# Differential attention: a second set of score banks for a head's second to fourth query tiles, and their minima ahead of the scaling

## The reference

```python
def diff_causal_attention(q, k, v, lam):
    '''q,k: (B,H,2,S,dq); v: (B,H,S,dv); lam: scalar float32. Returns (B,H,S,dv).'''
    scale = DIFF_QK_DIM ** -0.5
    for j in range(S_ // Q_BLOCK):
        lo, hi = j * Q_BLOCK, (j + 1) * Q_BLOCK
        s = jnp.einsum('bhmqd,bhmkd->bhmqk', q[:, :, :, lo:hi], k[:, :, :, :hi]).astype(jnp.float32) * scale
        mask = jnp.arange(hi)[None, :] <= jnp.arange(lo, hi)[:, None]
        p = jax.nn.softmax(jnp.where(mask, s, -jnp.inf), axis=-1)
        pd = p[:, :, 0] - lam * p[:, :, 1]
        outs.append(jnp.einsum('bhqk,bhkd->bhqd', pd.astype(v.dtype), v[:, :, :hi]))
```

## Time and profile before

| | |
|---|---|
| median of 3 runs | 3670.33 us (3666.89 to 3671.85) |
| profiled execution, own time | 3672.77 us |
| its span | 3671.0 us |
| TensorE matmul busy | 3372.6 us, 92% of the span |
| VectorE, ScalarE, GpSimd busy | 1344.2, 753.2, 1186.1 us |
| the attention stage | from 478.0 us (first scores) to 626.7 us (last products) |
| chain that ended last | TensorE 83%, VectorE 12%, ScalarE 3%, issue 2% |

### The profile page before, as it was taken

How to read it: one execution, slowest core, us unless ns; L and a number is a source line. 1 busy time by engine, 2 the same in 40 slices (tenths; PEclk the granted TensorE clock), 3 DMA queues, 4 the chain that set the end, 5 groups by cost and what they waited for, 6 DMA issues and landing times.

```text
span 3671.0 us, 37450 instructions
## 1 busy us (share of the span) xinstructions
PE 3372.6 (92%) x15576; PEld 2704.3 (74%) x15576; DVE 1344.2 (37%) x1653; ACT 753.2 (21%) x1091; POOL 1186.1 (32%) x996
## 2 busy tenths in 40 slices
PE   5967976889989899999999999998997899999997
PEld 4646855778868578878888888886984678888885
DVE  4145055133150540223451111217998662222223
ACT  2220045221120540111210000003442310010011
POOL 3200310325423023334444433343331344433341
PEclk9977999999989899999999999998998999999998
DMA  2100100102221001112111111111111011111111
GB/s 112 54 15 21 46 24 12 58 24 73 77 98 48 11 24 46 58 46 93 47 46 46 46 57 46 46 46 73 49 67 48 24 46 46 46 57 46 46 46 46
DMA packets 31742, 179.63 MB, mean 49 GB/s; under 512 B 3840, under 2 KB 4864, under 8 KB 14720
## 3 DMA queue, kind: packets, MB, share of 16 engines
q1 hardware_dynamic: 18864, 137.37, 10.6%
q10 hardware_dynamic: 12752, 40.42, 2.9%
HBM read 163.10 MB, written 14.68 MB: 48 GB/s over the span
## 4 chain that ended last, share of the span: by engine, by line
PE 83%; DVE 12%; ACT 3%; issue 2%; POOL 0%; DMA 0%; DVEq 0%; ACTq 0%
PE ps L441 48%; PE ps L472 16%; PE ps L498 5%; PE ps L1974 3%; DVE c_out L2398 2%; PE ps L1473 1%; PE ps L774 1%; PE ps L1489 1%; ACT p L944 1%; PE ps L682 1%; PE ps L2025 1%; DVE soft L1179 1%; PE ps L1459 1%; PE ps L321 1%; PE ps L329 1%
## 5 line engine op out<-in xcount | busy, mean ns | idle before, releaser
L538 POOL TENSOR_TENSOR whi<-raw,par 128x512 fp32r<-128x512 f32 x117 | 128.7, 1100 | 1939.3 <-PE ps L441 1477.9
L542 POOL TENSOR_TENSOR wlo<-raw,whi 128x512 fp32r<-128x512 f32 x468 | 695.5, 1486 | 37.3
L441 PE MATMUL ps<-xhi,whi 128*128 128x512 f32 x2016 | 631.7, 395 | 34.0 <-DVE xlo L344 9.5
L441 PE MATMUL ps<-xlo,whi 128*128 128x512 f32 x2016 | 626.6, 392 | 0.0
L441 PE MATMUL ps<-xhi,wlo 128*128 128x512 f32 x2016 | 625.0, 391 | 0.0
L441 PEld LDWEIGHTS ps<-xhi,whi 128*128 128x128 f32 x2016 | 379.8, 190 | 122.6 <-issue 11.9
L441 PEld LDWEIGHTS ps<-xlo,whi 128*128 128x128 f32 x2016 | 382.1, 190 | 81.3
L441 PEld LDWEIGHTS ps<-xhi,wlo 128*128 128x128 f32 x2016 | 381.3, 189 | 81.4
L540 POOL CAST whi<-raw 128x512 fp32r<-128x512 f32 x351 | 279.2, 795 | 0.0
L472 PE MATMUL ps<-hidden_lo,whi 128*128 128x512 f32 x864 | 268.9, 393 | 0.0
L472 PE MATMUL ps<-hidden_hi,whi 128*128 128x512 f32 x864 | 268.3, 392 | 0.4 <-DVE hidden_lo L1334 0.4
(11 more groups left out here) (480 smaller groups left out, 4588.4 us busy)
## 6 DMA issues: line engine op xcount, KB each, us to landing
raw<-stream SPq DMA_DIRECT2D x131, 1024.0 KB, 4.7
x_in<-xT ACTq DMA_DIRECT2D x4, 1024.0 KB, 14.7
x_again<-xT ACTq DMA_DIRECT2D x4, 1024.0 KB, 8.6
h_scr<-x_again ACTq DMA_DIRECT2D x4, 1024.0 KB, 4.3
h<-h_scr ACTq DMA_DIRECT2D x1, 4096.0 KB, 14.6
h_scr<-h ACTq DMA_DIRECT2D x4, 1024.0 KB, 4.7
outT<-h ACTq DMA_DIRECT2D x8, 512.0 KB, 3.0
bias<-bias ACTq DMA_DIRECT2D x1, 2560.0 KB, 9.5
```

Of the source, the lines that this page charges most:

```text
L441: mm = nc.tensor.matmul(ps[:, c0 + c:c0 + c + width], w, x(k, a, width), start=(n == 0 and m == 0), stop=(n == len(ks) - 1 and m == 2))
L538: nc.gpsimd.tensor_tensor(WHI[:, r, t], RAW[:, r, t], one, ALU.mult).then_inc(hi_done, 1)
L542: ins = nc.gpsimd.tensor_tensor(WLO[:, r, t], RAW[:, r, t], WHI[:, r, t].bitcast(F32), ALU.subtract)
```

## The change

The scores of the second to fourth tile of a head (j = 1, 2, 3; n is at most 512, one bank) get places of their own: tiles 2 and 4 in banks 1 and 3, tile 3 in banks 0 and 2 as the first. With this the TensorE wait in front of them is for the exponentials of the tile before the last, and on VectorE their minima are written ahead of the scaling of the tile in front. Tiles 1 and 5 to 8 are as they were. The numbers of instructions stay the same.

```diff
+        def ahead(i):
+            return STEPS[i][1] in (1, 2, 3)
+
+        def scores_at(i, m):
+
+            return 2 * BANK * m + (BANK if STEPS[i][1] in (1, 3) else 0)
...
-                    wait(pe, S("d_exp"), 2 * i)
+
+                    wait(pe, S("d_exp"), 2 * (i - 1 if ahead(i) else i))
...
-                            mm = nc.tensor.matmul(ps[:, 2 * BANK * m + c:2 * BANK * m + c + w], QT[rows, h, P * j:P * (j + 1)],
+                            mm = nc.tensor.matmul(ps[:, scores_at(i, m) + c:scores_at(i, m) + c + w], QT[rows, h, P * j:P * (j + 1)],
...
-                        e = 2 * BANK * m + n - P
+                        e = scores_at(i, m) + n - P
...
-                        nc.scalar.activation(buf[:, 0:n], ps[:, 2 * BANK * m:2 * BANK * m + n], ACT.Exp,
+                        nc.scalar.activation(buf[:, 0:n], ps[:, scores_at(i, m):scores_at(i, m) + n], ACT.Exp,
...
+            def minima(i):
+                n = P * (STEPS[i][1] + 1)
+                for m in range(2):
+                    dve.wait_ge(S("d_scores"), 2 * i + m + 1)
+                    nc_v.tensor_reduce(SM[:, i % 4, 2 + m:3 + m], ps[:, scores_at(i, m):scores_at(i, m) + n], AX, ALU.min)\
+                        .then_inc(S("d_nm"), 1)
+
             for i in range(n_steps + 2):
+                if i < n_steps and ahead(i):
+                    minima(i)
                 if 1 <= i <= n_steps:
...
-                if i < n_steps:
-                    n = P * (STEPS[i][1] + 1)
-                    for m in range(2):
-                        dve.wait_ge(S("d_scores"), 2 * i + m + 1)
-                        nc_v.tensor_reduce(SM[:, i % 4, 2 + m:3 + m], ps[:, 2 * BANK * m:2 * BANK * m + n], AX, ALU.min)\
-                            .then_inc(S("d_nm"), 1)
+                if i < n_steps and not ahead(i):
+                    minima(i)
```

## The result

The changed kernel takes **3692.97 us** (median, 3688.93 to 3696.0), the kernel before 3669.37 us in the same comparison: ratio 1.0063, 95% interval 1.005 to 1.0076, so 23.6 us slower. Forecast were 3680.7 us (+10.4) and a range from 3674.5 to 3689. The direction held, the size is more than double, and the time lies above the range.

What follows compares the result with a forecast made beforehand. In the attention stage a ring of scores, minima, exponentials and next scores was taken to bound the kernel. Heads 2 to 4 (+8.5) and the first head (+1.9) gave +10.4 on 3670.33: 3680.7 us, range 3674.5 to 3689.

Steps and rivals of the forecast that it cites:

- The ring: Heads 2 to 4: next scores wait for minima, scaling, transposes and products in turn; +2.82 us each, +8.5 us together.
- The first head: First head, partly at 1.2 GHz: third tile's scores 1.1 us earlier, fifth's later; +1.9 us.
- the rival in which it doesn't: TensorE stays at 2.4 GHz in the first head, saving 2.5 us there; +6.0 us, 3676.3 us, chance 0.13.
- The banks: Matmuls writing one bank while its neighbour is read cost 0, at worst 0.1 us for each of 12 tiles.
- The clock in heads 2 to 4: Rival: longer TensorE pauses bring 1.2 GHz in heads 2 to 4; +6.6 us more, 3687.3 us, chance 0.17.
- The sum: Attention stage: 8.5 us for heads 2 to 4 plus 1.9 for the first head, +10.4 us.
- two such tiles in each head: Two tiles at the low clock in each of heads 2 to 4, +6.6 us together.
- the old ring: Order before the change: scores, minima, exponentials, next scores; a low-clock tile costs 0.9 to 1.1 us in it.
- the new one: Changed order: scores, both minima, scaling, transposes, products, next scores; a low-clock tile costs up to 1.9 us.
- The signs: Forecast wrong if transposes don't wait for the next minima, stage isn't 8 to 13 us longer, or time changes behind it.
- The median before: Base of the forecast: 3670.33 us, the median of three runs; the profiled execution was 2.4 us above it.

Runs made afterwards that it cites:

- the filled kernel: The changed kernel with idle matmuls on TensorE before the transposes of tiles 1 to 3 of each head; 3677.81 us, ratio 1.0023.

## Why the prediction was wrong

**The ring: right.** From the earlier trace rows it gave 4.58, 3.66 and 4.60 us for the second, third and fourth tile, 12.84 in all. The third head of the first profile has 4.71, 3.73 and 4.67, the filled kernel 12.97 in all. Too small by 0.1 to 0.3 us a head: the order costs 8.9 us by the filled kernel, 8.5 were forecast. The second tile gained nothing, as forecast; its step lost 1.4 us, the third's 0.6 and the fourth's 1.0 (third head against the earlier trace rows). The fifth tile's ring stayed whole (575.10 to 579.32, 4.22 us, 4.22 before).

**The first head: right.** +1.9 forecast, +1.88 measured (38.70 us to the second head for 36.82). The clock fell there although two tiles' scores now come in one piece; the rival in which it doesn't is out. With idle matmuls it didn't fall, and the head was 1.8 us shorter than before (34.99 for 36.82), where that rival had 2.5.

**The banks: right.** Nothing was taken, and alone they change nothing that can be measured. By the rule of the Trainium skill (Perfetto Trace Analysis, section Matmuls) rotating banks should have helped; here they gave 0.5 us a head while the minima stayed behind the scaling. With the minima moved they gave nothing in heads 2 to 4 (13.1 us with and without them) and 1.9 us in the first (38.7 for 40.6).

**The clock in heads 2 to 4: this step failed.** The sum took these heads at 2.4 GHz throughout, as the earlier trace rows shows them, so its term for falls there was nothing. The prediction had them among the rivals with a chance of 0.17 and a price of "two such tiles in each head", +6.6 us, and set the range's upper end by it. It is what happened, in both profiles of the changed kernel, and it costs more. The stage is 22.2 and 25.2 us longer; less 8.9 for the order and 1.9 for the first head, the falls in heads 2 to 4 cost 11.4 and 14.4 us in these two executions. The medians say the same: 3693 to 3678 with idle matmuls is 15 us, of which 3.7 are the first head's. Two things were mis-sized. The chance: pauses of 1.45 to 2.25 us with little work between them were taken as probably harmless, because the earlier trace rows had pauses to 1.35 without a fall (1.44 in front of the first tile, in the line shown above), though the earlier trace rows had a fall with pauses of 2.1. And the price: six tiles at 1.1 us, which is what a low clock cost in the old ring. The same passage has up to 1.9 for the new one, and by its own terms for the first head a third tile costs 1.3 there (4.93 for 3.66, without the 0.3 for sharing with GpSimd) and a fourth 1.9 (6.47 for 4.60), which is 9.4 us in three heads and not 6.6. The rival's time would then have been 3690.

What the runs showed is also more than two tiles a head. A fall goes on into what TensorE does next. Where that is the 14 products of the previous head's seventh tile, the second tile comes 5.8 to 6.7 us after the first and not 4.36 (five times in the two profiles). Where it is the 16 of the eighth tile, the third comes 5.8 to 6.2 us after the second and not 4.7. And from the fourth to the fifth tile it takes 5.7 to 6.5 us for 4.7.

The Trainium skill's warning of idle gaps between bursts (TensorE: Matmul & The Clock Gate, section Why this matters for your kernels) names longer gaps than those in front of the falls of heads 2 to 4, and by it they should have been safe. The traces don't agree: the clock fell at 528 us behind a pause of 1.85 us. The forecast kept its 0.17 against this rule because of the earlier trace rows, and the runs bear out.

**The signs.** The prediction called itself wrong if the stage, to its last products, was not 8 to 13 us longer. It was 22 us longer (170.8 us from first scores to last products in the first profile, 148.7 before).

**The median before.** The sum was put on the median of three runs, rightly: that moved by 1 us. But the profile of before had no fall in heads 2 to 4, while that of the same code with idle matmuls in its first head alone had one; a profile shows the clock of one execution.

## What to carry to other kernels

Before an instruction is moved ahead of another on an in-order engine, write down who waits for the one that is passed, and what stands behind that waiter in its own queue: here the passed scaling released transposes, and the next scores stood behind them. A change that lengthens TensorE's pauses has a second price, the clock's, which can exceed the first; it can be separated from it with idle matmuls that fill the pauses. For a latency ring of a few us, compare the same interval in several heads and profiles at a known clock, since single executions of one kernel lie further apart than such a gain (3662.2 to 3677.0 us with the banks alone).

## What the runs showed of the hardware

- TensorE's clock fell to 1.2 GHz behind pauses of 0.92 and 1.45 us (at 521.4, changed kernel) and behind a single one of 1.85 us (at 528.2), and elsewhere stayed up through the same pattern (the third head's 1.45, 1.85 and 2.25). The same code with the same tile times kept 2.4 GHz in two heads and lost it in the third (idle matmuls in the first head of before: 34.65, 34.65 us, then a fall at 581.6 behind pauses of 1.45 and 0.92). So pauses of this length went with falls in some heads and not in others; what decides in the single case wasn't tried.
- Once low, the clock can stay low across pauses: in the first head of the changed kernel it was at 1.2 GHz from 478 to 497 us with TensorE busy for 12.3 of the 19 us. In the second head it was back at 524.8, behind the products that follow the fall at 521.4 without a pause.
- Adding 87 idle matmuls, 22.6 us of TensorE's busy time by the profile (12 in a row took 2.98 us), made the changed kernel 15 us faster.
